# A hybrid decoder layer: output projections' last units by thirds, prompt attention scaled by POOL with transposed outputs

## The chip, the cores and the metric

The kernel runs on one core of one Trainium2 chip. The metric is the device time of one launch in microseconds (us); of several runs the median is taken. A core has five engines with queues of their own: PE (TensorE, matmuls; its weight loads are listed as PEld), DVE (VectorE), ACT (ScalarE), POOL (GpSimd) and SP (SyncE, which issues DMAs here). They meet through semaphores. The profile comes from one further execution.

## The reference

One layer of a decoder for 1024 prompt positions and 8 x 8 sample positions, width 1024, all in f32, in a frame of residual sums:

```python
x = x + 0.5 * (silu(h @ wg) * (h @ wu)) @ wd            # ffn1, h = rmsnorm(x)
q, k, v, a, g = split(rmsnorm(x) @ w_in)
A = dilated sliding-window attention, 8 heads of 64, branches (128,1), (512,4), (2048,16), ALiBi
B = swish(layernorm(causal depthwise conv of a * sigmoid(g)))
x = x + [A | B] @ w_out
x = x + cross_attention(rmsnorm(x) @ w_cq, memory) @ w_co   # 4 heads of 256 over 256 memory tokens
x = x + 0.5 * ffn2(rmsnorm(x));   y = rmsnorm(x, final_norm)
```

An attention output is `sum(p * v) / sum(p)` with `p = exp(score + bias - max)`; the three branches of A are merged by their sums. What the change touches is the prompt's attention A and the products with w_out and w_co.

## The kernel before

**Products.** Every weight and activation is split in a high and a low part in a reduced type (fp32r), and a product is three matmuls per 128 rows, `three` (L963 to L965): high by high, low by high, high by low. POOL makes both parts of the weights (L788 and L790 for units of 128 x 1024, L796 and L798 for cuts of 128 x 512 of the ffn weights). x, its norm h and the parts hh and hl are feature-major, 8 rows of 128 features (k) by 1088 tokens, and the tokens are taken in thirds of 384, 384 and 320 (`CHUNKS`). One product is one unit of 128 output features (w) for one third (c): 24 matmuls over 8 k.

**Output projections.** `out_proj` runs w_out and w_co: units w from 0 to 7, in each the three thirds, 24 products in four PSUM banks by turns. DVE adds each result to x (L2451), ACT squares it (L1937), DVE sums the squares over w (L2460). PE sums over partitions with a matrix of ones, once for each third (`row_sum`, L1150 and L1152): for third 0 inside the last product but one, for thirds 1 and 2 after the last product. Behind each row sum stand ACT's root (L1948) and DVE's reciprocal (L2483); then eight tiles for the third: DVE multiplies x by gain and reciprocal (L2490), ACT rounds that to hh (L1953), DVE subtracts to get hl (L2467). `tail_order` (L428) is the common order of ACT and DVE: last adds, then the tiles of third 0, of third 1, of third 2. POOL's splits of the next weights wait for a slot, which is free when PE has finished the unit's last third (`unit_done`).

**The stages behind them.** After w_out comes `query_proj` (w_cq: i, then thirds, then four units), whose first results ACT copies out when tiles of third 1 are done (`copy_queries`). After w_co comes `ffn2`: units w, thirds c, gate and up products f; the first silu (L1691) on ACT is queued behind all of ACT's tiles; DVE then goes on with differences and products for the ffn (L2270, L2325, L2337, L2343).

**Prompt attention.** For two pairs of heads and again two (i), 16 steps n follow, a block of 128 queries each, head h inner. A step: PE's scores (L1353 near, L1359 far classes); DVE's mask with the row minimum (L2691); ACT's exp with its sum (L2100), into Sb (128 queries by 128 to 448 keys); PE turns Sb with an identity (`turn`, L1370); ACT copies the bank to PT (L2083); PE multiplies with the values (`values`): for whole blocks PT is the stationary operand and vtok moves 64 columns (L1383), for cuts of classes 16 small ones (L1389). DVE takes the reciprocal (L2698), scales the output to O2 (L2701), PE turns O2 (`turn_output`, L1405) and DVE copies it to oT (L2712). In step n PE runs scores(n+1), turn(n, 0), turn_output(n-2), values(n-1), turn(n, 1). On POOL only `sort_classes` runs here (L920): 12 copies that sort the queries, keys and values of a pair into classes (L931, L937); it waits for the pair's loads, the bias among them. SP loads four units of w_out behind attention's loads (L642).

## Time and profile before

| | |
|---|---|
| median of 3 runs | 2571.97 us (2570.71 to 2573.04) |
| the profiled execution | 2569.81 us |
| its span | 2568.0 us |
| mean granted TensorE clock | 0.988 |
| PE busy in the span | 2474.9 us (96%) |
| DVE, ACT, POOL busy | 1206.5, 658.5, 1199.5 us |
| DMA, mean over the span | 88 GB/s |

The span runs from the first to the last instruction of the profiled execution. Its stages by the timeline, in us from its start: prompt attention 1084.6 to 1211.5; samples' attention to 1368; w_out 1369.4 to 1472; w_cq to 1570; cross attention to 1699; w_co 1700.3 to 1800; ffn2 to 2536; the final norm to the end. Busy time says how long an engine worked, not whether anyone waited for it: that is read from the waits and the timelines of a stretch.

### The profile page before, as it was taken

Reading aid. Unit: us, or ns where it says so; the run is one execution under the profiler, and the core shown is the slowest. Engines: PE = TensorE matmul, PEld = TensorE weight load, DVE = VectorE, ACT = ScalarE, POOL = GpSimd, SP = SyncE. Lnnn points to the kernel's source line nnn. Section 1 sums busy time; section 2 is a strip of 40 time slices with the busy share of each in tenths; the row PEclk is TensorE's granted clock in tenths of the full one; section 3 lists DMA queues with packets and bytes.
Section 4 is the critical chain, followed back from the end, with each engine's and each line's share of the span. In section 5 each row is a group of like instructions: output and inputs, shape, how many; then the busy total and the mean of one; then the engine's idle time right before and its main releaser. Section 6 shows DMA issues by size and latency. Waiting matters only on the chain.

```text
span 2568.0 us, 48261 instructions
## 1 busy us (share of the span) xinstructions
PE 2474.9 (96%) x17695; PEld 2331.9 (91%) x17695; DVE 1206.5 (47%) x2551; ACT 658.5 (26%) x1671; POOL 1199.5 (47%) x1110
## 2 busy tenths in 40 slices
PE   7999999999999999999999999899899999999998
PEld 7999999999999999766558999679799999999997
DVE  5653333333336799434433433533953333333335
ACT  4321111111113233365222223321321111111113
POOL 7466666666666345022001220213176666666662
PEclk9999999999999999999999999999999999999999
DMA  7211111111112122354864113741011111111112
GB/s 244 90 46 45 46 45 45 47 46 49 49 50 74 42 67 76 115 171 132 348 235 135 50 68 129 290 145 42 17 53 47 45 45 49 45 45 45 45 49 95
DMA packets 216000, 224.78 MB, mean 88 GB/s; under 512 B 12090, under 2 KB 183670, under 8 KB 211795
## 3 DMA queue, kind: packets, MB, share of 16 engines
q1 hardware_dynamic: 199399, 195.46, 23.5%
q10 hardware_dynamic: 16492, 27.82, 3.0%
q8 instruction: 74, 1.21, 0.2%
q14 instruction: 35, 0.29, 0.0%
HBM read 190.84 MB, written 32.40 MB: 87 GB/s over the span
## 4 chain that ended last, share of the span: by engine, by line
PE 91%; DVE 5%; ACT 2%; DMA 1%; issue 1%; ACTq 0%; DVEq 0%; SPq 0%
PE ps L963 26%; PE ps L964 26%; PE ps L965 25%; PE ps L1451 2%; PE ps L1495 1%; PE ps L1465 1%; PE ps L1370 1%; PE ps L1383 1%; PE ps L1561 1%; DMA cK<-in_cache_mem_k 1%; PE ps L1544 1%; DVE ps L2490 1%; PE ps L1353 1%; DVE hl L2467 0%; PE ps L1389 0%
## 5 line engine op out<-in xcount | busy, mean ns | idle before, releaser
L963 PE MATMUL ps<-hh,wh 128*128 128x272 f32 (+2 forms) x2528 | 781.2, 309 | 16.6 <-ACT gated L1691 7.1
L965 PE MATMUL ps<-hl,wh 128*128 128x272 f32 (+2 forms) x2528 | 779.3, 308 | 0.0
L964 PE MATMUL ps<-hh,wl 128*128 128x272 f32 (+2 forms) x2528 | 779.2, 308 | 0.0
L798 POOL TENSOR_TENSOR wl<-raw,wh 128x512 fp32r<-128x512 f32 x384 | 496.1, 1292 | 30.7
L963 PEld LDWEIGHTS ps<-hh,wh 128*128 128x128 f32 x2528 | 478.9, 189 | 23.4 <-ACT gated L1691 7.4
L796 POOL CAST wh<-raw 128x512 fp32r<-128x512 f32 x384 | 235.3, 613 | 530.1 <-PE ps L965 460.8
L964 PEld LDWEIGHTS ps<-hh,wl 128*128 128x128 f32 x2528 | 478.0, 189 | 0.5
L965 PEld LDWEIGHTS ps<-hl,wh 128*128 128x128 f32 x2528 | 477.4, 189 | 0.0
L2354 DVE SCALAR_TENSOR_TENSOR x<-ps,x 128x384 f32<-128x384 f32 (+1 forms) x528 | 279.9, 534 | 196.8 <-PE ps L965 194.7
L788 POOL CAST wh<-raw 128x1024 fp32r<-128x1024 f32 x52 | 55.7, 1072 | 627.1 <-PE ps L965 425.0
L963 PE MATMUL ps<-hidh,wh 128*128 128x384 f32 (+1 forms) x1056 | 345.5, 327 | 0.6 <-DVE x L2354 0.5
L965 PE MATMUL ps<-hidl,wh 128*128 128x384 f32 (+1 forms) x1056 | 344.5, 326 | 0.0
L964 PE MATMUL ps<-hidh,wl 128*128 128x384 f32 (+1 forms) x1056 | 344.1, 326 | 0.0
L963 PE MATMUL ps<-th,wh 128*128 128x272 f32 x960 | 276.3, 288 | 3.0 <-ACT gated L1720 3.0
L964 PE MATMUL ps<-th,wl 128*128 128x272 f32 x960 | 277.2, 289 | 0.0
L965 PE MATMUL ps<-tl,wh 128*128 128x272 f32 x960 | 275.9, 287 | 0.0
L828 POOL TENSOR_TENSOR raw<-raw 128x512 f32<-128x512 f32 x160 | 206.7, 1292 | 0.0
L963 PEld LDWEIGHTS ps<-hidh,wh 128*128 128x128 f32 x1056 | 198.3, 188 | 2.0 <-issue 1.0
L964 PEld LDWEIGHTS ps<-hidh,wl 128*128 128x128 f32 x1056 | 198.2, 188 | 0.3
L965 PEld LDWEIGHTS ps<-hidl,wh 128*128 128x128 f32 x1056 | 198.2, 188 | 0.0
L2394 DVE TENSOR_TENSOR ps<-ps,parts 128x272 f32<-128x272 f32 x120 | 53.8, 448 | 307.0 <-PE ps L965 307.0
L2394 DVE TENSOR_TENSOR gated<-ps,gated 128x272 f32<-128x272 f32 x120 | 53.0, 442 | 300.5 <-PE ps L965 300.5
(278 smaller groups left out, 3318.2 us busy)
## 6 DMA issues: line engine op xcount, KB each, us to landing
raw<-in_ffn_gate SPq DMA_DIRECT2D x88, 256.0 KB, 2.9
raw<-in_ffn_up SPq DMA_DIRECT2D x88, 256.0 KB, 2.9
raw<-in_ffn_down SPq DMA_DIRECT2D x88, 256.0 KB, 2.7
Kw<-in_cache_win_k SPq DMA_DIRECT2D x24, 512.0 KB, 5.9
Vw<-in_cache_win_v SPq DMA_DIRECT2D x24, 512.0 KB
raw<-in_w_in SPq DMA_DIRECT2D x20, 512.0 KB, 3.8
Kw<-in_cache_win_k SPq DMA_DIRECT2D x8, 1024.0 KB, 8.6
Vw<-in_cache_win_v SPq DMA_DIRECT2D x8, 1024.0 KB
```

Source lines behind the costliest of these rows:

```text
L788: pool.tensor_copy(hi, src).then_inc(w_hi, 1)
L796: pool.tensor_copy(ring_hi(r), quadrant(q)).then_inc(s["whi"], 1)
L798: pool.tensor_tensor(ring_lo(r), quadrant(q), ring_hi(r).bitcast(F32), ALU.subtract).then_inc(s["lo"], 1)
L828: pool.tensor_tensor(out, a, b, op).then_inc(s["mix"], 1)
L963: pe.matmul(out, w_hi_, a_hi, start=first, stop=False, skip_group_check=more)
L964: pe.matmul(out, w_lo_, a_hi, start=False, stop=False, skip_group_check=more)
L965: return pe.matmul(out, w_hi_, a_lo, start=False, stop=last, skip_group_check=more)
L1353: mm = pe.matmul(ps[:, 2 * h + n % 2, far(t):far(t) + near(t)], qs[64 * h:64 * h + 64, 1 - p, t * P:(t + 1) * P], kTp[64 * h:64 * h + 64, ...
L1370: mm = pe.transpose(ps[0:w, b, k * P:(k + 1) * P], Sb[:, n % 2, h, c:c + w], ident[:])
L1451: mm = pe.transpose(ps[:, bank, m * P:(m + 1) * P], Kw[q % 2][:, n, k * P:(k + 1) * P], ident[:])
L2354: dve.scalar_tensor_tensor(out=x[:, d, c0:c0 + n], in0=ps[:, bank(j), 0:n], scalar=0.5, in1=x[:, d, c0:c0 + n], op0=ALU.mult, op1=ALU.add) ...
L2394: dve.tensor_tensor(out(c), ps[:, bank + c, 0:CW], kept(c), ALU.add).then_inc(s["part"], 1)
```

## The change

**Output projections.** `out_order` replaces the unit-by-unit order from unit 4 on: products 0 to 11 are as before, then come units 4 to 7 for third 0 (products 12 to 15), for third 1 (16 to 19) and for third 2 (20 to 23). The row sum of third 0 stands inside product 16, that of third 1 inside product 20, that of third 2 in the next stage: before the fourth query product, or after the second product of ffn2. `out_tail` replaces `tail_order`: "x" is a product's add, square and add of squares, "inv" root and reciprocal, "tiles" a run of tiles. ACT's first work for the next stage (three query banks copied; the first two silus) stands right behind the last root, ahead of tiles 16 to 24. `query_proj` and ACT's copies are written out accordingly.

**Prompt attention.** POOL multiplies Sb by the reciprocal of its sum before the turn (`scale`), with the 12 sort copies placed between its steps; DVE takes one reciprocal per head; PE's values swap their operands: values stationary, PT moving, and the result is the transposed output, which DVE copies from its bank; O2 and turn_output go. ACT runs both exps of a step behind the first copy of PT.

**Loads.** SP issues two of w_out's first four loads where it issued four, and the other two after the samples' loop.

The diff's core (hunks of data layout, of wiring of the stages, and lines that only rename are left out; of the last two hunks, DVE's and ACT's tails, only the lines after the change stand):

```diff
@@ -425,18 +425,23 @@
-    def tail_order():
-        seq = [("add", 0, 0), ("root", 0, 0), ("inv", 0, 0), ("add", 1, 0)]
-        for c in range(NC):
-            for k in range(KT):
-                seq.append(("tile", c, k))
-                if c == 0 and k == 2:
-                    seq.append(("add", 2, 0))
-                if c < NC - 1 and k == 4:
-                    seq.append(("root", c + 1, 0))
-            if c < NC - 1:
-                seq += [("lo", c, KT - 1), ("inv", c + 1, 0)]
+    def out_order():
+        return [(w, c) for w in range(4) for c in range(NC)] + [(w, c) for c in range(NC) for w in range(4, KT)]
+    def out_part(w, c):
+        return 2 * w + c + 1 if w < 4 else 8 + 4 * c + w - 4 + 1
+    def out_adds(q):
+        return sum(1 for w, c in out_order()[:q + 1] if 0 < w < KT - 1)
+    def out_tail():
+        seq = [("x", 15), ("inv", 0), ("x", 16), ("tiles", 0, 4), ("x", 17), ("tiles", 4, 8), ("x", 18), ("x", 19),
+               ("inv", 1), ("x", 20), ("tiles", 8, 12), ("x", 21), ("tiles", 12, 16), ("x", 22), ("x", 23), ("inv", 2),
+               ("tiles", 16, 24)]
...
@@ -639,7 +644,8 @@
-        first_loads("w_out")
+        for j in range(2):
+            load_unit(j, UNIT["w_out"] + j + 1, W["w_out"][:, :, j * P:(j + 1) * P])
...
@@ -673,6 +679,8 @@
+        for j in range(2, SLOTS):
+            load_unit(j % 2, UNIT["w_out"] + j + 1, W["w_out"][:, :, j * P:(j + 1) * P])
...
@@ -920,26 +928,45 @@
-        def sort_classes():
+        def attention():
...
-            for i in range(H // 4):
-                for p in range(2):
+            def sort(i, p, m):
+                src, dst = ((qT, qs), (kTp, kc), (vT, vc))[m]
+                if m == 0:
...
-                    for src, dst in ((kTp, kc), (vT, vc)):
-                        if p == 0 and dst is kc:
-                            pool.wait_ge(unit_done, SLOTS + COL["w_out"])
-                            pool.sem_inc(met, 1)
-                        pool.tensor_copy(dst[:, p].rearrange("c (r s) -> c r s", r=DIL),
-                                         src[:, p].rearrange("c (s r) -> c r s", r=DIL)).then_inc(A["sorted"], 1)
+                    return
+                if p == 0 and m == 1:
+                    pool.wait_ge(unit_done, SLOTS + COL["w_out"])
+                    pool.sem_inc(met, 1)
+                pool.tensor_copy(dst[:, p].rearrange("c (r s) -> c r s", r=DIL),
+                                 src[:, p].rearrange("c (s r) -> c r s", r=DIL)).then_inc(A["sorted"], 1)
+            def scale(i, n, h):
+                w = far(wsteps[n][1]) + near(wsteps[n][1])
+                pool.wait_ge(A["r"], i * (2 * WN) + (2 * n + h + 1))
+                pool.tensor_scalar(Sb[:, n % 2, h, 0:w], Sb[:, n % 2, h, 0:w], stat[:, n % 4, 2, h:h + 1], None,
+                                   ALU.mult).then_inc(A["p"], 1)
+            for m in range(3):
+                sort(0, 0, m)
+            for i in range(H // 4):
+                for n in range(WN):
+                    for h in range(2):
+                        scale(i, n, h)
+                    if 2 <= n < 5:
+                        sort(i, 1, n - 2)
+                    if i + 1 < H // 4 and 11 <= n < 14:
+                        sort(i + 1, 0, n - 11)
...
-                sort_classes()
+                attention()
...
@@ -978,9 +1005,12 @@
-                if 4 <= j < 10:
+                if j < 4:
+                    if out is not None:
+                        pe.wait_ge(out["free"], out.base["free"] + 4 + NC * KT - 4 + j + 1)
+                elif j < 10:
...
-                elif j >= 10:
+                else:
...
@@ -1067,6 +1097,8 @@
+                        if beside_first is not None and (w, c, f) == (0, 0, 1):
+                            beside_first()
...
@@ -1141,42 +1173,40 @@
+        def row_sum(sn, c):
+            n, q = CHUNKS[c][1], out_order().index((KT - 1, c))
+            pe.wait_ge(sn["var"], sn.base["var"] + out_adds(q))
+            pe.matmul(ps[:, 5 + c, 0:n], ones[:], sums[:, c, 0:n], start=True, stop=False)
+            pe.wait_ge(sn["sq"], sn.base["sq"] + q + 1)
+            pe.matmul(ps[:, 5 + c, 0:n], ones[:], sq[:, q % 4, 0:n], start=False, stop=True).then_inc(sn["summed"], 1)
...
-            def row_sum(c):
-                n, j = CHUNKS[c][1], NC * (KT - 1) + c
-                pe.wait_ge(sn["var"], sn.base["var"] + NC * (KT - 3) + c + 1)
-                pe.matmul(ps[:, 5 + c, 0:n], ones[:], sums[:, c, 0:n], start=True, stop=False)
-                pe.wait_ge(sn["sq"], sn.base["sq"] + j + 1)
-                pe.matmul(ps[:, 5 + c, 0:n], ones[:], sq[:, j % 4, 0:n], start=False, stop=True
-                          ).then_inc(sn["summed"], 1)
-            for w in range(KT):
-                pe.wait_ge(w_split, u0 + w + 3)
-                for c, (c0, n) in enumerate(CHUNKS):
-                    j = w * NC + c
-                    pe.wait_ge(s["free"], s.base["free"] + j + 1)
-                    out = ps[:, j % 4, 0:n]
-                    for k in range(KT):
-                        if w == 0:
-                            pe.wait_ge(s["h"], s.base["h"] + KT * c + k + 1)
-                        mm = three(out, unit_hi(w % 4)[:, k], unit_lo(w % 4)[:, k], hh[:, k, c0:c0 + n], hl[:, k, c0:c0 + n],
-                                   k == 0, k == KT - 1)
-                        if k == 4 and j == NC * KT - 2:
-                            row_sum(0)
-                    mm.then_inc(s["part"] if c < NC - 1 else unit_done, 1)
-            for c in range(1, NC):
-                row_sum(c)
+            for q, (w, c) in enumerate(out_order()):
+                c0, n = CHUNKS[c]
+                if c == 0:
+                    pe.wait_ge(w_split, u0 + w + 3)
+                pe.wait_ge(s["free"], s.base["free"] + q + 1)
+                for k in range(KT):
+                    if w == 0:
+                        pe.wait_ge(s["h"], s.base["h"] + KT * c + k + 1)
+                    mm = three(ps[:, q % 4, 0:n], unit_hi(w % 4)[:, k], unit_lo(w % 4)[:, k], hh[:, k, c0:c0 + n],
+                               hl[:, k, c0:c0 + n], k == 0, k == KT - 1)
+                    if k == 5 and q in (16, 20):
+                        row_sum(sn, c - 1)
+                mm.then_inc(s["part"] if c < NC - 1 else unit_done, 1)
...
-            with pe.Fori(0, KT // 4) as i:
+            for i in range(KT // 4):
...
+                        if (i, c, w) == (0, 0, 3):
+                            row_sum(s, NC - 1)
...
@@ -1364,7 +1394,7 @@
-                pe.wait_ge(A["e"], i * (2 * WN) + (2 * n + h + 1))
+                pe.wait_ge(A["p"], i * (2 * WN) + (2 * n + h + 1))
...
@@ -1380,15 +1410,16 @@
-                        mm = pe.matmul(ps[:, 6 + n % 2, 64 * h:64 * h + 64], PT[:, n % 2, h, len(cuts) + k, :],
-                                       vtok[:, p, t + 1 - len(whole) + k, 64 * h:64 * h + 64], start=(k == 0 and h == 0),
+                        mm = pe.matmul(ps[64 * h:64 * h + 64, 6 + n % 2, 0:P],
+                                       vtok[:, p, t + 1 - len(whole) + k, 64 * h:64 * h + 64],
+                                       PT[:, n % 2, h, len(cuts) + k, :], start=(k == 0),
...
-                    for h in range(2):
-                        for r in range(DIL):
-                            mm = pe.matmul(ps[FAR * r:FAR * (r + 1), 6 + n % 2, 64 * h:64 * h + 64],
-                                           PT[0:w, n % 2, h, k, FAR * r:FAR * (r + 1)],
-                                           vfar[0:w, p, 2 * r + k, 64 * h:64 * h + 64], start=False,
+                    for r in range(DIL):
+                        for h in range(2):
+                            mm = pe.matmul(ps[64 * h:64 * h + 64, 6 + n % 2, FAR * r:FAR * (r + 1)],
+                                           vfar[0:w, p, 2 * r + k, 64 * h:64 * h + 64],
+                                           PT[0:w, n % 2, h, k, FAR * r:FAR * (r + 1)], start=False,
...
@@ -1420,14 +1445,10 @@
-                if n >= 2:
-                    turn_output(n - 2)
...
-            turn_output(WN - 2)
...
-            turn_output(WN - 1)
...
@@ -2124,8 +2155,9 @@
-                    if n + 1 < WN:
-                        exp(n + 1, h)
+                    if n + 1 < WN and h == 0:
+                        exp(n + 1, 0)
+                        exp(n + 1, 1)
...
@@ -2693,14 +2734,9 @@
-            def normalise(n):
-                dve.wait_ge(A["e"], i * (2 * WN) + (2 * n + 2))
-                dve.reciprocal(stat[:, n % 4, 2, :], stat[:, n % 4, 1, :]).then_inc(A["r"], 1)
-                dve.wait_ge(A["r"], i * WN + (n + 1))
-                dve.wait_ge(A["v_full"], i * WN + (n + 1))
-                dve.tensor_tensor(O2[:, n % 2], ps[:, 6 + n % 2, 0:P].rearrange("p (h e) -> p h e", e=HD),
-                                  stat[:, n % 4, 2, :].unsqueeze(2).to_broadcast([P, 2, HD]), ALU.mult
-                                  ).then_inc(A["scaled"], 1)
+            def inverse(n, h):
+                dve.wait_ge(A["e"], i * (2 * WN) + (2 * n + h + 1))
+                dve.reciprocal(stat[:, n % 4, 2, h:h + 1], stat[:, n % 4, 1, h:h + 1]).then_inc(A["r"], 1)
...
@@ -2721,12 +2759,11 @@
-                if n >= 2:
-                    output(n - 2)
+                if n + 1 < WN:
+                    for h in range(2):
+                        inverse(n + 1, h)
...
-                    normalise(n - 1)
-            output(WN - 2)
-            normalise(WN - 1)
+                    output(n - 1)
...
@@ -2467,32 +2505,35 @@
+            add_square(14)
+            for what, a, *b in out_tail():
+                if what == "x":
+                    add(a)
+                    add_square(a)
                 elif what == "inv":
+                    n = CHUNKS[a][1]
+                    dve.wait_ge(sn["std"], sn.base["std"] + a + 1)
+                    dve.reciprocal(rs[:, a, 0:n], rs[:, a, 0:n]).then_inc(sn["rstd"], 1)
+                else:
+                    for j in range(a, b[0]):
+                        c, k = divmod(j, KT)
+                        c0, n = CHUNKS[c]
+                        if k == 0:
+                            dve.wait_ge(sn["rstd"], sn.base["rstd"] + c + 1)
+                            dve.wait_ge(s["free"], s.base["free"] + 4 + 16 + 4 * c)
+                        if j >= 2:
+                            dve.wait_ge(sn["h"], sn.base["h"] + j - 1)
+                        dve.scalar_tensor_tensor(out=ps[:, 4 + j % 2, 0:n], in0=x[:, k, c0:c0 + n],
+                                                 scalar=vecs[:, gain + k:gain + k + 1], in1=rs[:, c, 0:n],
+                                                 op0=ALU.mult, op1=ALU.mult).then_inc(sn["t"], 1)
+                        if k >= 1:
+                            lo(j - 1)
+                    if b[0] % KT == 0:
+                        lo(b[0] - 1)
...
@@ -1927,54 +1948,64 @@
+            for what, a, *b in out_tail():
+                if what == "x":
+                    square(a)
+                elif what == "inv":
+                    n = CHUNKS[a][1]
+                    act.wait_ge(sn["summed"], sn.base["summed"] + a + 1)
+                    act.activation(rs[:, a, 0:n], ps[:, 5 + a, 0:n], ACT.Sqrt, bias=eps, scale=1.0 / D
                                    ).then_inc(sn["std"], 1)
+                    if a == NC - 1 and beside_last is not None:
                         beside_last()
+                else:
+                    for j in range(a, b[0]):
+                        c, k = divmod(j, KT)
+                        c0, n = CHUNKS[c]
+                        act.wait_ge(sn["t"], sn.base["t"] + j + 1)
+                        act.copy(hh[:, k, c0:c0 + n], ps[:, 4 + j % 2, 0:n]).then_inc(sn["hi"], 1)
...
+        def begin_queries():
+            for w in range(3):
+                copy_query(0, 0, w)
```

## Rows read from the trace of the kernel before

**Rows 1.** The page, part 4: the chain that ended last, by engine

```profile
PE 91%; DVE 5%; ACT 2%; DMA 1%; issue 1%; ACTq 0%; DVEq 0%; SPq 0%
```

**Rows 2.** Stretches: us, busy (count) of PE, PEld, DVE, ACT, POOL; PEclk; DMA; GB/s

```profile
1084.60:1211.50 126.90, 114.01 (x1580) 85.14 (x1580) 53.13 (x231) 80.47 (x221) 32.27 (x18) 0.97 0.48 154
1131.19:1134.41 3.22, 3.22 (x52) 2.39 (x52) 1.69 (x8) 2.09 (x6) 0.00 (x0) 1.00 0.40 163
1472.43:1491.43 19.00, 18.70 (x96) 18.04 (x97) 17.44 (x28) 8.19 (x18) 0.00 (x0) 0.91 0.10 28
1522.14:1538.81 16.67, 16.67 (x98) 16.67 (x97) 0.00 (x0) 1.87 (x4) 5.92 (x4) 1.00 0.40 131
1800.08:1839.04 38.96, 29.09 (x144) 25.89 (x145) 36.13 (x69) 15.60 (x34) 3.06 (x4) 0.87 0.01 1
1821.51:1824.92 3.41, 0.66 (x4) 0.34 (x2) 3.01 (x7) 1.41 (x4) 0.00 (x0) 1.00 0.00 0
1824.92:1835.16 10.24, 5.92 (x22) 5.92 (x23) 9.57 (x24) 5.60 (x13) 0.00 (x0) 0.50 0.00 0
1827.90:1894.40 66.50, 63.69 (x385) 63.12 (x385) 63.67 (x149) 18.43 (x47) 29.86 (x30) 0.95 0.12 35
```

**Rows 3.** PE's waits over the span: who for, total us, times, longest

```profile
PE ps L963 <- ACT gated L1691: 7.1, 1, 7.1
...
PE ps L1405 <- DVE O L2701: 1.1, 2, 0.6
```

**Rows 4.** Timeline of an attention step: start, us, engine, line, operation [idle before]

```profile
1132.15 0.55 PE L1370 MATMUL ps<-ident,Sb 128*128 128x128 f32 x3
...
1132.48 0.53 DVE L2691 CUSTOM_DVE_ANT_0 Sb<-ps,qkvb 128x352 f32<-128x352 f32 x1 [1.14 <-PE ps L1359]
1132.54 0.27 PE L1405 MATMUL ps<-ident,O 128*128 128x128 f32 x1
...
1132.64 1.00 PE L1383 MATMUL ps<-vtok,PT 128*128 128x64 f32 x8
...
1133.16 0.59 ACT L2100 ACTIVATE Sb<-Sb,stat 128x352 f32<-128x352 f32 x1
...
1133.58 0.42 PE L1389 MATMUL ps<-vfar,PT 32*32 32x64 f32 x16
1133.60 0.15 DVE L2698 RECIPROCAL stat<-stat 128x2 f32<-128x2 f32 x1
...
1133.93 0.55 PE L1370 MATMUL ps<-ident,Sb 128*128 128x128 f32 x3
```

**Rows 5.** Groups of POOL's instructions: line, form, count | busy us, mean ns | idle before

```profile
L798 POOL TENSOR_TENSOR wl<-raw,wh 128x512 fp32r<-128x512 f32 x384 | 496.1, 1292 | 30.7
L796 POOL CAST wh<-raw 128x512 fp32r<-128x512 f32 x384 | 235.3, 613 | 530.1 <-PE ps L965 460.8 <-POOL raw L828 25.6 <-DMA raw<-in_ffn_up 21.7
```

**Rows 6.** Timeline of PE in the samples' attention

```profile
1247.50 0.39 PE L1468 MATMUL ps<-Kc,Qc 128*64 128x128 f32 x4
...
1247.72 0.24 PE L1471 MATMUL ps<-Kt,Qc 128*64 128x8 f32 x4
```

**Rows 7.** Timeline of POOL in attention: a sort behind the bias

```profile
1101.45 2.09 POOL L931 COPY qs<-qkvb 128x1024 f32<-128x1024 f32 x1 [16.25 <-DMA qkvb<-in_prompt_bias]
```

**Rows 8.** Timelines of the two norm tails and of the head of ffn2

```profile
1463.61 2.55 DVE L2483 RECIPROCAL rs<-rs 128x384 f32<-128x384 f32 x1 [3.94 <-ACT rs L1948]
...
1469.32 2.54 POOL L790 TENSOR_TENSOR wl<-raw,wh 128x1024 fp32r<-128x1024 f32 x1
...
1470.44 1.84 DVE L2490 SCALAR_TENSOR_TENSOR ps<-x,vecs,rs 128x384 f32<-128x384 f32 x1
...
1472.88 0.63 DVE L2490 SCALAR_TENSOR_TENSOR ps<-x,vecs,rs 128x384 f32<-128x384 f32 x1
...
1827.94 0.45 DVE L2270 TENSOR_TENSOR ps<-hh 128x272 f32<-128x272 f32 x1
...
1894.39 0.39 PE L963 MATMUL ps<-th,wh 128*128 128x272 f32 x1 [1.48 <-ACT gated L1720]
```

156 lines of the change are left out of this document (64 added, 92 removed).

## The prediction

> **What bounds the kernel now.** I read the page first: of the chain that ended last, TensorE (PE) holds 91% [rows 1], so time is won only where PE idles, runs slowly, or has work removed. Next the stretches by engine around each place the change touches [rows 2], for PE's idle time and its clock; then PE's waits [rows 3], for what ended that idle time; last the timelines of one attention step and of the two norm tails [rows 4, 8]. The profiled execution took 2569.81 us (2568.0 in its span), 2.2 less than the median of the three runs, 2571.97; the sum is made on 2569.8, and 2.2 is added back.
>
> Three places lose or hold time. Prompt attention lasts 126.90 us with PE busy for 114.01. From the end of w_co to the end of ffn2's sixth product 38.96 us go by [rows 2]. Four products of 384 columns take 16.67 us where nothing disturbs them, so 4.17 each and 3.47 for 320 columns; six cost 23.6, and 15.3 are lost: 7.1 is one wait on the first silu [rows 3], about 3 is the clock, which stands at 0.50 for 10.24 us after 3.41 us in which PE was busy for only 0.66 (its lower level, 1.2 GHz) [rows 2], and the rest are waits for h. At the head of w_cq 19.00 stands against 16.67, plus 1.2 for the row sums still due after w_out: 3.5 to 4 lost.
>
> **Attention: what PE loses and gains.** The step at 1131.19 lasts 3.22 us and PE is busy for all of it [rows 2]: scores 0.96, turn 0.39, turn_output 0.10 (1132.54 to 1132.64), value blocks 0.94 (1132.64 to 1133.58), cuts 0.35, second turn 0.48 [rows 4]. The change removes turn_output. The eight block products get a 128x64 stationary operand and write one half of the partitions each. The nearest rows are the samples' scores with the same stationary shape and 128 moving columns: four issued in 0.22 us (1247.50 to 1247.72), pairs side by side [rows 6]; eight cost 0.43 instead of 0.94. The 16 cuts get w x 64 stationary operands and 32 moving columns; no row has that, and I take 0.43 against 0.35 (bounds: 0.16 less, if they too overlap, to 0.4 more, if each load is exposed). Together 0.52 less: a step of 2.70.
>
> **Attention: the new chain.** Before, the reciprocal stood beside PE's path; now each turn waits for mask, exp, VectorE's (DVE's) reciprocal and a POOL multiply. From the start of the scores (1131.19) to the mask 1.29, mask 0.53, exp 0.59 with its reads and hand-overs 0.25, reciprocal 0.23 with its wait, POOL 0.48, hand-overs 0.10: 3.47 us [rows 4]. The scores are issued 0.96 ahead of the previous turn, so the chain asks for 2.51 a step at 352 columns. Wider steps ask more (about 2.6 at 384, 2.7 at 416): PE stays the bound, barely. POOL's price is the open term. Bounds: its cast, also one input and one output, 613 ns for 512 columns, so 0.42 at 352 by width, and its two-input subtraction, 1292 ns, so 0.9 [rows 5]. I take the cast, with some fixed share, 0.48, for the scale also reads one tile and a column.
>
> **Attention: the sorts.** POOL's 12 copies are 2.1 us each [rows 7], ran beside everything, and now stand between scales on the same queue. A step with a sort costs POOL 2.1 + 2 x 0.48 and hand-overs, 3.1 to 3.3: those nine steps (2 to 4 of either pair, 11 to 13 of the first) stay at the old pace. The other 23 save about 0.45 on average (0.52 in a full one, less in the first steps, which have one block): 10.4. The sort in step 2 waits for the transfer of the second pair's bias, whose landing released POOL at 1101.45 [rows 7]. Before, the queries' sort alone stood behind that; now scale(3,0) does too: 1101.45 + 2.09 + 0.5 = 1104.05, about 2.4 later than PE asks for turn(3,0). At the two ends a wait on the scaled output goes, 1.1 in all [rows 3]. PE idles more per step than before, which may cost one stretch of low clock: 0.8. Sum: 10.4 - 2.4 + 1.1 - 0.8 = **8 gained**, bounds 2 and 11. SP's two w_out loads that move behind the samples, and POOL's splits of them, cost nothing: POOL splits w_out only behind attention in either order, w_out begins some 158 us later, and POOL is free in between. The masks ran beside the sorts before too.
>
> **Output projections: w_co into ffn2.** Count from the end of product 15 (t = 0). By the trace that is 1764.4: w_co's end at 1800.08 less eight products (31.3) and the row sums. The first row sum comes at 3.1, its root at 4.6, the reciprocal (2.55 [rows 8]) to 7.8, tiles of third 0 at some 1.2 each (0.63 [rows 8] and the subtraction) to 20.3 with the adds between them. The adds and squares 18 and 19 end at 22.8; PE wants the second row sum at 20.6 and waits: 1.6 to 1.7 new. Products 20 to 23 end from 24.4 on, each freeing a slot, and POOL splits a cut of ffn2 then (0.61 + 1.29 [rows 5]). DVE operations with two inputs in SBUF stop beside those: 1.84 us instead of 0.63 [rows 8]. So tiles 8 to 15 end at 43 and not 39; the last row sum, wanted at 43.2, waits for 1.7; the third root is at 46.4, the last tile at 57.8, that is 1822.2. The silus now stand ahead of tiles 16 to 24, so the 7.1 us wait goes, and so do the first tile waits and the low clock: PE is up to 15 us earlier for six products. But what is late next is DVE: from the end of its tiles (1827.94) it is busy for 63.67 of 66.50 us, and at the end PE waits for it (1894.39) [rows 2, 8]. Only what DVE's tiles advance counts there: 1827.9 - 1822.2 = 5.7; PE's earlier products just wait for hid. I take **5.2 gained** (bounds 3, and 7.6 if POOL doesn't disturb DVE).
>
> **Output projections: w_out into w_cq.** The same order; here no DVE chain follows, and PE's own stalls count. Before: 3.9 lost. After: row sum 1 waits for 1.65; from t = 24.4 POOL splits whole units (some 3.6 us each, 2.54 of it the subtraction [rows 8]) beside DVE's tiles; the add and square 22 and 23 come at 45.8 where PE's third query product (row sum 2 before the fourth, slots freed by the adds) wants them at 43.2: 2.6; and one stretch at low clock, 1.7. That is 5.9: **1.9 lost** (bounds: 2.4 gained without the contention; 4 lost).
>
> The Trainium skill, SBUF — State Buffer, "SBUF: two separate sides", says that a DVE operation reading two SBUF operands and a GpSimd one exclude each other, the loser waiting for the whole instruction; the pair at 1469.32 and 1470.44 agrees [rows 8]. By it the splits' new place beside the tail costs what is set above; without it the sum would be about 7 better, which is rival 3.
>
> The Trainium skill, GPSIMD Engine Reference, "Engine selection", would put this elementwise scale on VectorE; of its reason, that two-input work is about twice as slow on GpSimd, 613 and 1292 ns show the same [rows 5]. If the scale pays so, rival 1 is the result.
>
> **Sum.** 2569.8 - 8 - 5.2 + 1.9 = 2558.5; with 2.2 added, 2560.7: **2561**.
>
> **Rivals.** 1: the scale costs POOL the two-input price. A plain step's chain becomes 3.47 + 0.44 - 0.96 = 2.95, so it gains little; a sort step costs POOL 2.1 + 1.8 + 0.2 = 4.1, 0.9 over the old pace, nine times. Attention is then about 2.5 slower than before instead of 8 faster: 2571.5. For: the chain has almost no room (2.51 against 2.70). Against: one input.
> 2, the slower side: the same steps with PE falling to 1.2 GHz. The place is the nine sort steps and those behind them; PE has some 2.3 us of work in a step of 4.1; the mechanism is what stands at 1821.51, where PE idled and ran at 0.50 for the next three times as long [rows 2]. Price: half speed for some 20 us of PE work, about 10: 2581. It decides once a scale of 352 columns takes more than 0.9 us; at 0.48 not.
> 3: POOL's splits don't disturb the tails: 2.4 + 4.3 better, 2554.5.
> 4: attention turns out bound by the chain of hand-overs through three engines (0.2 each more than set), so plain steps keep 3.1 and only the ends and a little are won: 2567.
> 5: the change doesn't do what it says in the tails: DVE's tiles, now between adds that PE waits for, leave PE stalling in the output products themselves, w_co gains nothing and w_out loses 6: 2570.5.
>
> **How the numbers follow.** The forecast 48% (2561; its own bounds 2555 to 2567), rival 1 15%, rival 2 9%, rival 3 9%, rival 4 11%, rival 5 8%. A measurement of this kernel tells about 0.2%, 5.1 us, from no change: faster is under 2566.8, slower over 2577.1. Faster: most of the forecast, rival 3 and half of rival 4, 0.60; slower: rival 2 and a part of 1 and 5 that comes out worse, 0.14; same 0.26. The range goes from 2552 to 2575: it leaves out rival 2 and the outer ends of rivals 1 and 3, some 2 in 10.
>
> **What would show it.** Attention from 126.9 to about 119; L1405's row gone; plain steps at 2.7 us, sort steps at 3.2; POOL's scale of 352 columns at 0.48 us; PE waiting on POOL about 2.4 us near 1102. In the tails: 1.65 us waits of PE at the row sums of third 1, a DVE tile of 1.8 us beside POOL's splits, no wait on the first silu, DVE's last tile of w_co 5 to 6 us earlier relative to product 15, PE's wait in ffn2's second unit for hid. Wrong would make it: a scale over 0.6 us, a lower PEclk inside attention, cuts over 0.8 us, or DVE's chain in ffn2 not holding PE.

## The result, and the profile after

The changed kernel took 2585.56 us (median of 5 runs, 2579.04 to 2590.39) against 2571.97 before (median of 5 then, 2569.39 to 2576.01): a ratio of 1.0056, 95% interval 1.0041 to 1.0071. (A ratio here and below compares all runs of a kernel with those of the kernel before, taken beside them; it need not be the quotient of the two medians to the last digit.) It is 13.6 us slower. The forecast was 2561, faster, with a range up to 2575. The profiled execution is the slowest of the five, 2590.39 us (span 2588.4), 20.6 us over the profiled execution before, so the losses read in its trace are larger than those of the median.

The page shows two of it at once, the path (part 4) and POOL's busy time (part 1, which was 1199.5 before):

```profile
PE 2484.6 (96%) x17663; PEld 2333.1 (90%) x17663; DVE 1214.1 (47%) x2551; ACT 657.8 (25%) x1671; POOL 1269.4 (49%) x1174
...
PE 88%; DVE 6%; ACT 2%; issue 1%; POOL 1%; DMA 1%; ACTq 0%; DVEq 0%; SPq 0%
```

TensorE (PE) has 10 us more busy time with 32 instructions fewer, and POOL stands on the path with 1%, where it had nothing [rows 1]. The same stretches as in [rows 2], columns as there: prompt attention; three sort steps of its second part; the head of ffn2 behind w_co, into its sixth product; the later place where the clock falls.

```profile
1086.14:1235.60 149.46, 126.63 (x1548) 85.06 (x1548) 53.10 (x229) 79.50 (x221) 92.30 (x77) 0.84 0.38 123
1178.29:1194.59 16.30, 14.67 (x153) 9.06 (x151) 5.54 (x23) 6.89 (x20) 13.84 (x11) 0.62 0.11 34
1826.26:1849.85 23.59, 23.59 (x138) 22.93 (x139) 20.20 (x36) 9.46 (x20) 4.48 (x5) 1.00 0.10 32
1871.64:1878.47 6.83, 4.81 (x18) 4.81 (x19) 6.55 (x17) 2.10 (x5) 0.00 (x0) 0.50 0.00 0
```

Attention takes 149.46 us, with a mean clock of 0.84. Between 1178.29 and 1194.59 stand exactly three steps, 5.4 us each, where the step of [rows 2] had 3.22; POOL is busy for 13.84 of 16.30. The head of ffn2 runs without an idle moment at full clock, where 15 us were lost [rows 2]; the last line is where PE stands now, DVE busy for 6.55 of 6.83 us and the clock at 0.50 behind PE's new wait. Inside attention are two long stretches at 0.50 (PE's lower level, 1.2 GHz), one in each part:

```profile
1107.05:1124.10 17.05, 16.77 (x151) 10.60 (x151) 5.81 (x22) 6.12 (x18) 11.09 (x8) 0.50 0.09 20
1182.10:1199.20 17.10, 16.93 (x155) 10.66 (x152) 5.74 (x23) 7.06 (x20) 11.42 (x9) 0.50 0.01 2
```

PE's waits of the whole span, as in [rows 3]:

```profile
PE ps L1400 <- POOL Sb L953: 16.1, 17, 2.5
...
PE ps L990 <- DVE hidl L2379: 4.8, 1, 4.8
...
PE ps L990 <- DVE x L2487: 2.2, 1, 2.2
...
PE ps L1179 <- DVE sums L2498: 1.6, 2, 0.8
```

L1400 is the turn, L953 POOL's scale: 16.1 us in 17 waits. L2379 is the new wait in ffn2, L2487 the add before the third query product, L1179 the row sum of third 1, twice 0.8. Of the wait for the first silu (7.1) 0.3 is left, and that for the scaled output (1.1) is gone. And the price of one scale, by form:

```profile
L953 POOL TENSOR_SCALAR Sb<-Sb,stat 128x352 f32<-128x352 f32 x8 | 9.2, 1157 | 1.0 <-DVE stat L2739 1.0
```

1157 ns, where the prediction set 480 and bounded it by 900.

Where the 20.6 us are, by the traces. In the trace before, attention's first scores start at 1084.68 and PE's last instruction in it is the turn of an output at 1210.08:

```profile
1210.08 0.30 PE L1405 MATMUL ps<-ident,O 128*128 128x128 f32 x1 [0.57 <-DVE O L2701]
```

That is 125.7 us (the stretch of [rows 2], 126.90, reaches 1.1 us further, into the samples' part), and it is 149.5 now: 23.8 more. From w_out's first product to the end of the fourth query product 122.2 us became 122.8, though the first product of the kernel before took 0.8 more, at half clock: some 1.4 lost. From w_co's first product to the last product ahead of the final norm 835.6 us became 828.9: 6.7 gained. The other 2 us are differences ahead of attention and around the samples.

### The profile page after: what moved, and what is told of

Its sections match the earlier page's. It is cut to its first block, busy times and chain, and to the rows that moved or that the text cites. A ratio compares the mean times of both kernels' runs of the same rounds, so it can differ in the third digit from the quotient of the medians.

```text
span 2588.4 us, 48126 instructions
## 1 busy us (share of the span) xinstructions
PE 2484.6 (96%) x17663; PEld 2333.1 (90%) x17663; DVE 1214.1 (47%) x2551; ACT 657.8 (25%) x1671; POOL 1269.4 (49%) x1174
## 4 chain that ended last, share of the span: by engine, by line
PE 88%; DVE 6%; ACT 2%; issue 1%; POOL 1%; DMA 1%; ACTq 0%; DVEq 0%; SPq 0%
PE ps L990 25%; PE ps L991 25%; PE ps L992 25%; PE ps L1472 2%; PE ps L1516 1%; PE ps L1486 1%; PE ps L1400 1%; PE ps L1582 1%; POOL Sb L953 1%; PE ps L1565 1%; DVE ps L2530 1%; DVE ps L2306 1%; DMA cK<-in_cache_mem_k 1%; PE ps L1420 1%; PE ps L1413 1%
## 5 line engine op out<-in xcount | busy, mean ns | idle before, releaser
L836 POOL TENSOR_TENSOR raw<-raw 128x512 f32<-128x512 f32 x160 | 206.7, 1292 | 0.0
```

Of the source, the lines that this page charges most:

```text
L836: pool.tensor_tensor(out, a, b, op).then_inc(s["mix"], 1)
```

## The experiments

The theory after this reading: **A**, POOL's price. A scale costs 1.16 us at 352 columns and not 0.48, so a sort step needs 2 x 1.16 + 2.05 on one queue and more with the hand-overs. **C**, the clock: the starved steps pull PE down to 1.2 GHz, and that costs more than the waits. Against them **B**: the new chain over four engines, or the swapped products themselves, are slow, whatever POOL costs; and that the two halves disturb each other.

### The halves alone

`attention_only` takes only the attention hunks and the two moved loads into the kernel before; `tails_only` only the output projections.

> Only the attention half of the change, with its two moved loads; the output projections stay as before. In the changed kernel attention took 149.5 us against 126; POOL's scale of 352 columns took 1157 ns, and TensorE stood at its lower clock for two stretches of 17 us in it. If attention alone carries the loss, this kernel is 18 to 24 us slower than the kernel before (about 2592), and attention lasts about 149. If the two halves disturb each other (loads, POOL's queue), it is well under 10 slower.

> Only the output projections' half. By the traces w_out with its tail lost about 1.4 us and w_co with ffn2 gained 6.7, so 5 us faster than before (about 2567). Rival: what was gained behind w_co comes from the shifted state of the changed kernel, and this is within 2 us of the kernel before.

Measured: attention alone 2590.16 against 2569.23, ratio 1.0078 (1.0065 to 1.0091), 20.9 us slower; the tails alone 2564.99, ratio 0.9981 (0.9972 to 0.9991), 4.2 faster. Both came as expected. The sum is 16.7 slower, the whole change 13.6, within what runs differ. The halves add up within the noise, and attention carries the loss. Its stretch in `attention_only`:

```profile
1084.41:1232.27 147.86, 123.99 (x1548) 84.06 (x1548) 52.11 (x228) 79.31 (x221) 92.96 (x78) 0.86 0.38 125
```

### POOL's price, down to nothing

Four kernels keep the whole change and alter only the scale. Each leaves out the normalisation or a part of it, so they tell about time alone. `scale_copy`:

```diff
-                pool.tensor_scalar(Sb[:, n % 2, h, 0:w], Sb[:, n % 2, h, 0:w], stat[:, n % 4, 2, h:h + 1], None,
-                                   ALU.mult).then_inc(A["p"], 1)
+                pool.tensor_copy(Sb[:, n % 2, h, 0:w], Sb[:, n % 2, h, 0:w]).then_inc(A["p"], 1)
```

`scale_32` has `w = 32`; `scale_constant` has `0.5` for the column of reciprocals; `swap_only` has no scale and no reciprocal, and the turn waits for ACT's exp (A["e"]) as before the change.

> The whole change, with POOL's scale cut to the first 32 columns of each row of probabilities (the other columns stay unscaled: part of the computation left out); waits, sorts and order stay. A scale then takes some 0.36 us by the line through the measured sizes (603 ns at 128, 1403 at 448). Theory A: attention falls to 119 to 124 us and the clock stays high in it; time about 2557 to 2562. Theory B: attention stays over 130. If the sorts between the scales were the main cause, sort steps stay at 3 us or more and attention at about 124 to 128.

> The whole change, with POOL's multiply replaced by a POOL copy of the same tile onto itself, same width, same waits (the scaling itself is left out). It tells whether the copy form has the price that the prediction gave the scale, 0.48 us at 352 columns, and what the rest of the prediction's model was worth. If only the price was wrong: copy 0.42 to 0.5 us at 352, attention about 118. If the model was wrong as well (the cuts of the swapped products cost 0.2 a step more than set, the turns 0.1): attention 122 to 126, time 2556 to 2563. If a copy of f32 costs as the multiply does: as the whole change, 2580 or more.

> The whole change, with POOL's multiply by a constant 0.5 instead of the column of reciprocals, everything else as it is (the normalisation by the sum is left out). It tells whether the price is the column operand's or the operation's. If the column makes it dear: as the copy, 0.48 us at 352 columns, attention about 124. If TENSOR_SCALAR itself is dear on POOL: 1.1 to 1.2 us, attention about 149.

> The whole change without any scale and without the reciprocals: the turn waits for ACT's exp as before; the swapped value products, POOL's sorts and both tails stay (the normalisation of the prompt attention is left out). With the copy in the scale's place attention took 123.6 us with TensorE idle for 13.4. If TensorE's own work is the bound there (it is about 107 at full clock), leaving the chain out changes little: attention 120 to 123. If the new chain through DVE and POOL binds even at the copy's price, attention falls to 116 to 119, and the time 5 or more under that of the copy (2562.6).

Measured: 2561.53 us for `scale_32` (ratio 0.9972, 0.9959 to 0.9985), 2562.64 for `scale_copy` (0.9957, 0.9942 to 0.9973), 2574.67 in one run for `scale_constant`, 2558.48 for `swap_only` (0.9961, 0.9948 to 0.9975). Their prices at 352 columns (`scale_32` at 32, all in one row), in the order scale_32, scale_copy, scale_constant:

```profile
L953 POOL TENSOR_SCALAR Sb<-Sb,stat 128x32 f32<-128x32 f32 x64 | 23.2, 366 | 76.0 <-DVE stat L2739 75.1
```
```profile
L953 POOL COPY Sb<-Sb 128x352 f32<-128x352 f32 x8 | 3.7, 480 | 1.6 <-DVE stat L2738 1.5
```
```profile
L953 POOL TENSOR_SCALAR Sb<-Sb 128x352 f32<-128x352 f32 x8 | 8.6, 1095 | 1.1 <-DVE stat L2739 1.1
```

The attention stretches of swap_only, scale_copy and scale_constant, one kernel to a fence (that of scale_32 lasts 123.3):

```profile
1087.47:1206.95 119.48, 109.01 (x1548) 75.29 (x1548) 45.41 (x164) 78.71 (x221) 26.34 (x14) 0.96 0.47 154
```
```profile
1087.22:1210.80 123.58, 110.20 (x1548) 75.43 (x1548) 51.69 (x228) 78.96 (x221) 51.68 (x78) 0.96 0.46 150
```
```profile
1087.49:1222.71 135.22, 110.99 (x1548) 75.48 (x1548) 51.73 (x228) 79.09 (x221) 86.49 (x77) 0.96 0.42 137
```

Three readings. First, theory A stands: with the same semaphores and sorts, the copy's price takes attention from 149.5 to 123.6. A price under 0.48 brings almost nothing more (123.3 at 0.37). Second, the copy costs 480 ns at 352 columns, the very figure of the prediction; what was wrong was that a multiply by a column costs as a copy. It isn't the column: with a constant it is still 1095 (the price was as expected; the attention of 149 expected with it was not, see below). The operation's form is dear on POOL. Third, the prediction's model was wrong too: with its own price attention should have been about 118 (125.7 less the 8 set), and it is 123.6; with no chain at all it is 119.5. So by these two traces about 4 us are the chain's hand-overs. The runs of the two kernels don't confirm it: their ratios, 0.9957 and 0.9961, are the same within their intervals, and 119.5 lies between the two outcomes named for `swap_only`. The swapped products bring far less than set. The step at 352 columns in `swap_only`, PE alone (it begins at 1132.54 with the scores and ends at 1135.62 with the next):

```profile
1132.54 0.70 PE L1375 MATMUL ps<-qkvb,qs 64*128 64x256 f32 x4
...
1133.50 0.55 PE L1392 MATMUL ps<-ident,Sb 128*128 128x128 f32 x3
...
1133.98 0.66 PE L1405 MATMUL ps<-PT,vtok 128*64 128x128 f32 x8
...
1134.56 0.65 PE L1412 MATMUL ps<-PT,vfar 32*64 32x32 f32 x16
...
1135.15 0.55 PE L1392 MATMUL ps<-ident,Sb 128*128 128x128 f32 x3
...
1135.62 0.70 PE L1375 MATMUL ps<-qkvb,qs 64*128 64x256 f32 x4
```

3.08 us from start to start, against 3.22 [rows 2, 4]: scores 0.96 as before, turn 0.48 (before 0.39, followed by 0.10 of turn_output: next to nothing is won there), blocks 0.58 (before 0.94), cuts 0.59 (before 0.35), second turn 0.47. The step gives 0.14, not the 0.52 of the prediction. The starts of the single instructions show why the cuts got dearer. Before, with 32 stationary columns, four ran side by side (they start within 0.02 us at 1133.58), and the next four began 0.06 to 0.08 behind them. With 64 stationary columns only two do (from 1134.56), and the pairs follow each other every 0.06: the same 16 cuts take twice as many turns.

### The clock apart from the waits

`filler` leaves the change as it is and gives PE spare work in the starved steps:

```diff
                 p, t = wsteps[n]
-                pe.wait_ge(A["p"], i * (2 * WN) + (2 * n + h + 1))
                 b = tbank()
+                if n in (3, 4, 5) or (i == 0 and n in (12, 13, 14)):
+                    for _ in range(6):
+                        pe.transpose(ps[:, b, 0:P], ident[:], ident[:])
+                pe.wait_ge(A["p"], i * (2 * WN) + (2 * n + h + 1))
```

> The whole change, with six spare transposes of the identity (128 x 128, about 0.12 us each) put on TensorE ahead of each turn of the nine steps that follow a sort, into the bank that the turn then overwrites; the result is unchanged. They fill time in which TensorE waits for POOL and shorten nothing. Theory C (three quarters of attention's loss is the clock, which fell because TensorE idled in these steps: 41 us more at the lower clock in the profile, about 18 us): the two 17 us stretches at 1.2 GHz go or shrink, attention falls from 149 to 131 to 137 though TensorE does 13 us more work, the time falls by 8 to 16 (about 2572). Rival D (POOL's price and the sorts alone set the steps, and the clock costs nothing because TensorE waits anyway): attention stays at 147 or more, no change in time.

Measured: 2579.98 us, ratio 1.0025 (1.0014 to 1.0037) against 1.0056 (1.0041 to 1.0071) for the change without it; the intervals don't meet. The attention stretch, and the two places of the 17 us stretches:

```profile
1087.54:1227.38 139.84, 121.13 (x1656) 86.35 (x1656) 51.55 (x228) 79.53 (x221) 91.55 (x77) 0.98 0.40 132
...
1107.00:1124.00 17.00, 16.61 (x226) 12.52 (x227) 6.73 (x29) 8.94 (x25) 13.49 (x10) 1.00 0.19 58
1182.00:1199.00 17.00, 16.64 (x235) 12.73 (x233) 6.02 (x29) 11.10 (x31) 10.42 (x9) 1.00 0.12 33
```

PE does 108 transposes more (108 x 0.12 = 13 us of work), and attention is 9.6 us shorter, with the clock at 0.98 instead of 0.84 and both long low stretches gone. The clock is what the extra work changed for the better; rival D (the clock is free because PE waits anyway) falls. The size was set too high: attention was expected at 131 to 137 and took 139.8, and the time fell by 5.6 us between the medians (8 by the ratios), where 8 to 16 were expected.

What the clock cost in the profiled execution follows from two traces with the same PE instructions: busy time 126.63 against 110.20 in `scale_copy`, 16.4 us, while the idle time rose by 9.4 (149.46 - 126.63 = 22.8 against 13.4). So of the 25.9 us between the copy and the multiply at most 16 are the clock: at full speed PE would have waited for POOL during a part of them. `scale_constant` bounds it from the other side: it idles about as long as the whole change (135.22 - 110.99 = 24.2), its price is only 5% lower (POOL is busy for 5.8 us less), but the long low stretches are absent and attention is 14 us shorter; that leaves 8 to 14 for the clock. This is one run, though. The five runs of the changed kernel part by the clock as well: 2585.56, 2588.21 and 2590.39 us at a mean clock of 0.982, 2579.04 and 2581.54 at 0.987. That the same waits sometimes lower the clock and sometimes not is likely from this, but only one of the five has a trace.

`sorts_spread` puts the sorts at every other step (n in (2, 4, 6) and (11, 13, 15)).

> The whole change, with POOL's sorts at every other step (behind steps 2, 4, 6 and 11, 13, 15) instead of behind three steps in a row. POOL has the same work, and it is late in every wide step, so the waits stay the same in sum. Theory C (a run of starved steps lowers the clock): TensorE's idle time is thinner, the two 17 us stretches at 1.2 GHz shrink to half or less, attention 134 to 142, time 5 to 12 lower than the whole change. Rival: the clock falls in any case for as long, attention stays at 147 to 150; or POOL is behind for longer and attention grows.

Measured: 2583.66 us, ratio 1.0057 (1.0043 to 1.0071), no different from the whole change. Its attention stretch, and the 17 us at half clock that are left in it:

```profile
1088.33:1232.25 143.92, 124.60 (x1548) 84.47 (x1548) 52.19 (x228) 79.41 (x221) 91.71 (x77) 0.85 0.39 129
...
1109.20:1126.20 17.00, 16.72 (x151) 10.54 (x149) 5.86 (x22) 6.13 (x18) 11.33 (x8) 0.50 0.10 20
```

The clock is 0.85 all the same. One of the two long stretches went (shorter ones came in its place), idle time went down by 3.5 us to 19.3, and 143.9 lies between what the theory and its rival set; but the expectation that spreading the sorts saves the clock, and 5 to 12 us with it, was wrong. What exactly about the starved steps lowers it stays open; only that work in their gaps prevents it is shown.

### Another engine, another form

`scale_dve` multiplies on VectorE (DVE), right behind the reciprocal. `scale_tt` keeps POOL and writes the multiply with two inputs, the column broadcast:

```diff
-                pool.tensor_scalar(Sb[:, n % 2, h, 0:w], Sb[:, n % 2, h, 0:w], stat[:, n % 4, 2, h:h + 1], None,
-                                   ALU.mult).then_inc(A["p"], 1)
+                pool.tensor_tensor(Sb[:, n % 2, h, 0:w], Sb[:, n % 2, h, 0:w],
+                                   stat[:, n % 4, 2, h:h + 1].to_broadcast([P, w]), ALU.mult).then_inc(A["p"], 1)
```

> The whole change, with the scale of the probabilities on VectorE instead of POOL, right behind the reciprocal; POOL only sorts. Theory A (POOL's price with its queue is the cause): the chain loses some 0.7 us a head, steps fall to 2.7 to 2.9 us, attention to 118 to 123, and the time to about 2557 to 2561. Theory B (the chain of hand-overs through ACT, DVE and PE binds, or the swapped value products are slow): steps stay at 3.2 or more and the time over 2567.

> The whole change, with POOL's multiply written as a two-input operation, the column of reciprocals broadcast along the row; the result is the same. By the price of POOL's other two-input operations (1292 ns for 512 columns) 0.9 us at 352 columns. If POOL's price sets waits and clock together: attention 126 to 132, clock nearly without low stretches, time 2563 to 2570, as much as 18 below the whole change. If the two-input form costs as the one with a column (1.1 us or more): attention 140 to 150.

Measured: `scale_dve` 2569.96 (ratio 0.9994, 0.9983 to 1.0006), `scale_tt` 2569.7 (1.0000, 0.9989 to 1.0011). Both take the whole loss back and win nothing: the 4 us of the tails are in them too, so by the runs their attention still costs about as much as that. First scale_tt's price and attention, then attention of scale_dve with two of its scales by form:

```profile
L953 POOL TENSOR_TENSOR Sb<-Sb,stat 128x352 f32<-128x352 f32 x8 | 6.0, 773 | 1.3 <-DVE stat L2739 1.3
```
```profile
1086.36:1213.00 126.64, 111.91 (x1548) 76.47 (x1548) 51.64 (x228) 78.93 (x221) 67.81 (x77) 0.95 0.44 146
```
```profile
1084.75:1217.25 132.50, 116.91 (x1548) 79.85 (x1548) 84.57 (x292) 79.77 (x221) 25.59 (x14) 0.90 0.43 140
```
```profile
L2734 DVE TENSOR_SCALAR Sb<-Sb,stat 128x256 f32<-128x256 f32 x8 | 7.7, 969 | 0.3
...
L2734 DVE TENSOR_SCALAR Sb<-Sb,stat 128x384 f32<-128x384 f32 x8 | 3.4, 421 | 0.3
```

The one-line edit to two inputs makes POOL a third cheaper (773 ns for 1157) and attention 22.8 us shorter. It was expected at 0.9, with 126 to 132 for attention. On DVE the scale costs 0.42 us at 384 columns, but a mean of 0.97 at only 256. The timeline of scale_dve shows why:

```profile
1129.95 2.07 POOL L947 COPY kc<-qkvb 128x1024 f32<-128x1024 f32 x1
...
1131.00 1.18 DVE L2734 TENSOR_SCALAR Sb<-Sb,stat 128x256 f32<-128x256 f32 x1
...
1131.96 2.13 POOL L947 COPY vc<-qkvb 128x1024 f32<-128x1024 f32 x1
...
1132.29 1.95 DVE L2734 TENSOR_SCALAR Sb<-Sb,stat 128x256 f32<-128x256 f32 x1
```

Beside a sort a scale lasts until the sort is over (scales end at 1132.18 and 1134.24, sorts at 1132.02 and 1134.09). The Trainium skill, SBUF — State Buffer, "Who interferes with whom", says that DVE's tensor_scalar can take the port pair that it shares with GpSimd, and that the second to come is held for the whole instruction; these rows agree. My expectation of 118 to 123 left this out, and attention took 132.5, with the clock at 0.90. The time, 2569.96, is even where theory B was to show itself (over 2567); that B isn't the cause is shown by `scale_32` and `scale_copy`, not by this run.

### The tails, taken apart

`hoist_only` is the kernel before with ffn2's first two silus moved ahead of the tiles of third 2 on ACT, nothing else. `wco_only` is the kernel before with the new order for w_co and ffn2 only.

> The kernel before, with only ffn2's first two silus moved on ACT from behind all tiles of w_co's norm to behind the tiles of its second third; order of products, row sums and tiles as before. Prediction's theory (DVE's tiles bound what follows, TensorE's wait for the silu is only moved): the 7.1 us wait goes from the head, TensorE waits 5 to 7 us more for hid later, time within 1.5 us of the kernel before. Rival (the silu wait itself was the loss): 5 to 7 us faster, so that this line alone is the tails' gain.

> The kernel before, with the output projections' half of the change for w_co and ffn2 only; w_out and w_cq in the old order. By the traces the new order behind w_out lost 1.4 us and behind w_co gained 6.7; with both 4.2 were gained. So 5 to 7 us faster than before (about 2564), 1 to 2 faster than both orders together. If w_out's order is neutral: 4.2 faster, as both.

Measured: `hoist_only` 2570.45 against 2571.59, ratio 1.0001 (0.9992 to 1.0010); `wco_only` 2563.69, ratio 0.9965 (0.9952 to 0.9979). In hoist_only PE's waits have, in the place of the 7.1 us for the silu [rows 3]:

```profile
PE ps L963 <- DVE hidl L2347: 4.8, 1, 4.8
```

The silu's wait goes and nothing is won: DVE's chain behind the tiles was what held the stage. The gain of the tails is that DVE's tiles end earlier. Whether the new order behind w_out costs anything isn't shown. 4.2 us are won with both orders and 7 to 8 with w_co alone, but the intervals of the ratios overlap (0.9972 to 0.9991 for `tails_only`, 0.9952 to 0.9979 and 0.9960 to 0.9981 for the two of w_co alone). In the trace of `tails_only` w_out's first product to the end of the fourth query product takes 122.1 us, as before (122.2).

### A version better than both

`best_split` is `wco_only` with the attention half, head 0 scaled by DVE and head 1 by POOL. `split_tt` is the same with POOL's two-input form, and `wco_again` repeats `wco_only` beside it on one chip.

> A version meant to beat both: w_out in the old order, w_co and ffn2 in the new one, and the attention half with head 0 scaled by VectorE (0.42 us at 352 columns in the run that scaled both there) and head 1 by POOL (1.16 us), whose turn comes one set of value products later. If POOL's one scale fits (2.06 + 1.16 + hand-overs is 3.4 in a sort step, nothing else is over 3), attention is 121 to 126 with little low clock, and the time 6 to 12 below the kernel before. If the sort steps still starve TensorE, attention is 128 to 135 and the time is that of the old attention or worse, 2566 to 2573.

> w_out in the old order, w_co in the new one, head 0 scaled by VectorE and head 1 by POOL, now in the two-input form. With the column form attention took 124.4 us, 1.3 less than before the change. At 0.9 us for POOL's scale it is 122 to 125; the time is 0 to 3 us below wco_again. If VectorE's scale, which took 0.9 to 1.2 us where it fell beside POOL's work, is what binds, attention stays at 124 to 126 and the time equals wco_again's within 1.5 us or is above it.

> The kernel with only w_co and ffn2 in the new order, once more, beside the one above on the same chip: 5 to 8 us faster than the kernel before, attention 125.5 to 126.5.

Measured: `best_split` 2565.64 (ratio 0.9985, 0.9975 to 0.9995), against 2569.48; `split_tt` 2561.66 (0.9962, 0.9950 to 0.9974) and `wco_again` 2564.39 (0.9970, 0.9960 to 0.9981) against 2571.39. `best_split` missed: its attention took 124.4 us, as expected, but it won 3.8 us and not 6 to 12, which is less than w_co's order wins alone. Attention of split_tt and of wco_again (the old form):

```profile
1085.20:1207.84 122.64, 109.85 (x1548) 75.48 (x1548) 67.47 (x260) 78.85 (x221) 45.97 (x45) 0.96 0.46 151
```
```profile
1084.66:1210.42 125.76, 114.08 (x1580) 85.08 (x1580) 52.37 (x228) 80.44 (x221) 32.22 (x18) 0.97 0.48 155
```

These two, as expected, beat the kernel before and the changed one. By the traces the repaired attention is worth 3.1 us; the two medians differ by 2.7, with intervals that overlap, so the attention half has at best a small gain, and most of what is to be had is w_co's order.

## Why the prediction was wrong, point by point

**The step that failed** is POOL's price. The prediction bounded a multiply by a column with the two rows that POOL had, a cast (613 ns for 512 columns) and a two-input subtraction (1292 ns) [rows 5], and took the cast because both have one input: 0.48 us. The multiply costs 1157 ns at 352 columns, outside both bounds (0.42 and 0.9): neither row was of the same operation, and the upper one was taken as an end it isn't. By `scale_copy` and `scale_32` this term with what follows from it is the whole loss: at 480 ns the same kernel is 9 us faster than before. The Trainium skill, GPSIMD Engine Reference, "Engine selection", calls one-input work on GpSimd roughly line-rate and two-input work about twice as slow as on VectorE. The copy comes near the first (480 ns at 352 columns, where VectorE's scale takes 415 in `scale_dve`), and the two-input form fits the second (773). The multiply by a scalar does not: with one input and a constant it still takes 1095.

**What followed was rival 2**, and it was on the right side with the right place: two scales and a sort on one queue, the point from which it decides (0.9 us), PE at 1.2 GHz. Its chance, 9%, was as small as it was because the bound was trusted. Its time, 2581, is 4.6 short of the median. It had attention 2.5 longer by waits and 10 by the clock, where the trace, of the slowest run, shows 23.8. With scale and sort in one step, three steps last 16.3 us, 5.4 each; the rival had 4.1 as POOL's time, reckoned with 0.9 and not 1.16 for a scale. It also counted half speed for 20 us; in the trace it is two stretches of 17 us and one of 7 beyond those of before.

**The second mis-sized term** is what PE saves. Predicted 0.52 a step, measured 0.14 with no chain (`swap_only`). The blocks save 0.36, not 0.51: pairs do run side by side and follow each other every 0.11 us, as set, but some 0.15 passes at the two ends of the group. Dropping turn_output gains 0.01, not 0.10, as the turn before it now takes 0.48 where it took 0.39. The cuts went from 0.35 to 0.59, set at 0.43; within the bounds, and the row they were set by had four cuts side by side, where the swapped ones ran two side by side. The new chain, at the price that was predicted, costs some 4 us in the traces (119.5 against 123.6), set at nothing: a part of rival 4. So with POOL's scale at 0.48, as set, attention gives 2 us in the trace (125.7 to 123.6), not 8.

**The sort behind the bias** came near by luck. Scale(3,0) was set to end at 1104.05, behind a sort that the bias's landing releases at 1101.45. It began at 1104.68, right behind the sort, but the sort had not waited for the bias: it began as POOL's two scales of step 2 ended. At the price that was set the wait is there, as the last line, of `scale_copy`, shows. PE's turn waited 1.5 in the change, set 2.4:

```profile
1100.74 1.98 POOL L953 TENSOR_SCALAR Sb<-Sb,stat 128x288 f32<-128x288 f32 x2 [2.49 <-DVE stat L2739]
...
1102.66 2.06 POOL L941 COPY qs<-qkvb 128x1024 f32<-128x1024 f32 x1
1104.68 2.16 POOL L953 TENSOR_SCALAR Sb<-Sb,stat 128x320 f32<-128x320 f32 x2
...
1103.09 2.05 POOL L941 COPY qs<-qkvb 128x1024 f32<-128x1024 f32 x1 [0.78 <-DMA qkvb<-in_prompt_bias]
```

**w_co into ffn2** was right in kind and somewhat small: 5.2 set, 6.7 in the trace (6.1 to 6.5 in those of `tails_only`, `wco_only` and `wco_again`), 7 to 8 in the medians of the last two. DVE's chain holds the stage, as claimed (`hoist_only`), and PE's new wait for hid is 4.8. Counted from w_co's first product, DVE's last tile comes 7.5 us earlier, set 5.7. The row sum of third 2 waited for almost nothing, set 1.7. That of third 1 costs about 1.4 over a quiet one, set 1.65: PE waits 0.8 ahead of its first instruction, and the second comes 1.02 behind the first, where in the quiet row sum of third 0 it comes 0.65 behind. Both in w_out:

```profile
1462.72 0.81 PE L1179 MATMUL ps<-sums,ones 128*128 128x384 f32 x2
1463.37 0.81 PE L1181 MATMUL ps<-sq,ones 128*128 128x384 f32 x2
...
1481.12 0.91 PE L1179 MATMUL ps<-sums,ones 128*128 128x384 f32 x2 [0.79 <-DVE sums L2498]
1482.14 0.91 PE L1181 MATMUL ps<-sq,ones 128*128 128x384 f32 x2
```

**w_out into w_cq** was right in its terms, but the loss is not certain: 1.9 lost was set, and 1.4 is in the trace of the change. The third query product waits for 2.2 (set 2.6), and a low stretch of 3.4 us follows (set 1.7 of cost, which is what half clock for 3.4 us takes). In the trace of `tails_only` the waits are the same (2.1 and 0.8), the clock stays at 1.00 behind them, and nothing is lost. What makes the adds late is POOL's splits beside DVE. The DVE lines are two tiles, one tile and one add of squares, and the POOL line is the split beside the second of them:

```profile
1487.90 4.08 DVE L2530 SCALAR_TENSOR_TENSOR ps<-x,vecs,rs 128x384 f32<-128x384 f32 x2
...
1492.95 2.58 POOL L798 TENSOR_TENSOR wl<-raw,wh 128x1024 fp32r<-128x1024 f32 x1
...
1493.78 2.17 DVE L2530 SCALAR_TENSOR_TENSOR ps<-x,vecs,rs 128x384 f32<-128x384 f32 x1
...
1497.35 2.65 DVE L2498 TENSOR_TENSOR sums<-sums,sq 128x320 f32<-128x320 f32 x1 [0.54 <-ACT sq L1962]
```

A tile takes 0.63 undisturbed [rows 8]. The sum of the tails, 3.3 us gained, met 4.2 measured. Had attention been left alone, that would have been the result (`tails_only`, 2564.99).

**Small slips in the sums.** The 126.90 us of attention held 1.1 us of the next part, so "about 119" should have been 118; 10.4 - 2.4 + 1.1 - 0.8 is 8.3, written as 8; and rival 3 should read 2554.3. None changes the outcome.

## What to carry to other kernels

Price an operation on POOL by a row of the same form, not by its number of inputs: here a copy, a two-input multiply and a multiply by a scalar took 480, 773 and 1157 ns for the same tile. When work moves from beside the critical engine into its chain, add up its new engine's whole queue for one step; if that exceeds the step, the waits are only part of the bill, since TensorE's clock can fall with them, as it did here (0.84), and then the work itself gets dearer. And before a wait is hoisted away, ask which engine is late next: taking the silu out of PE's way gave nothing until DVE's tiles ended earlier.

## What the runs showed of the hardware that was not expected

POOL's TENSOR_SCALAR on f32 costs about 2.5 ns for each further column (603 ns at 128 columns, 1403 at 448), hardly less with a constant (1095 for 1157 at 352); a two-input multiply whose second input is one column broadcast costs 1.67 ns a column (401 at 128, 934 at 448). Both stand on a fixed part of 0.2 to 0.3 us. Two full inputs cost somewhat more than the broadcast: in the trace of the change 464, 735 and 1289 ns at 128, 256 and 512 columns, against 401 and 614 at 128 and 256.

PE's spare transposes made a stage shorter: 13 us of added work, 9.6 us less time, since the clock stayed at 0.98.

Swapping the operands gained where the stationary one went from 128 to 64 columns and 128 move instead of 64 (0.94 to 0.58 us for eight): one at a time became two side by side. It lost where the stationary one went from 32 to 64 columns and 32 move instead of 64 (0.35 to 0.59 us for sixteen): four side by side became two.
